# A two-group encoder step on one core: memory projections moved from the front into 64 steps that the recurrence and the latent attention are laid between, with half-size weight chunks

## The reference, cut to what matters

```python
p_mem_k = einsum('bmd,lde->lbme', mem_prompt, xa_wk)     # both layers, also outputs
p_mem_v = einsum('bmd,lde->lbme', mem_prompt, xa_wv)
z = x @ w_in                    # u, gate, c_q, c_kv, k_pe
u_c = causal_conv(u); h = rg_lru(u_c)                    # gates, decay, scan over time
rec_out = h * gelu(gate)
q = rms_norm(c_q) @ w_uq; ckv = rms_norm(c_kv)           # rope on q_pe and k_pe
attn_out = latent attention of q on ckv (w_uk, w_uv), chunk mask, softmax
x = layer_norm(alpha * x + concat(rec_out, attn_out) @ w_out)
x = layer_norm(alpha * x + cross_attention(x, p_mem_k[l], p_mem_v[l]))
x = layer_norm(alpha * x + squared_relu_mlp(x))
```

## Time and profile before

| what | value |
|---|---|
| timed runs | 3116.03, 3117.30, 3129.95 us, median 3117.3 |
| profiled execution, first to last instruction | 3119.3 us |
| TensorE busy | 3036.5 us (97%), 20530 matmuls |
| VectorE busy | 1907.7 us (61%) |
| ACT, POOL busy | 413.1 and 92.4 us (13% and 3%) |
| mean granted TensorE clock | 0.987 |

### The profile page before, as it was taken

One profiled execution on the slowest core, in us unless ns is written; L12 is line 12 of the kernel. 1 busy time (PEld: TensorE's weight loads), 2 busy tenths in 40 slices (PEclk: granted clock), 3 DMA queues, 4 the chain that ended last, 5 costly groups with the idle time before them and its releaser, 6 DMA issues.

```text
span 3119.3 us, 47921 instructions
## 1 busy us (share of the span) xinstructions
PE 3036.5 (97%) x20530; PEld 2862.2 (92%) x20530; DVE 1907.7 (61%) x1485; ACT 413.1 (13%) x763; POOL 92.4 (3%) x64
## 2 busy tenths in 40 slices
PE   8999999899999999999999998999999999999998
PEld 6888899689989899999999996898999999999997
DVE  5666667646635766555565668744676555566565
ACT  2000003310220211000110003311031100011001
POOL 0000000100000000000000001000000000000000
PEclk9999999889999999999999999999999999999999
DMA  6666654234344355555555552453445555555542
GB/s 240 223 218 212 225 179 109 99 111 158 126 144 135 120 163 161 164 168 166 162 161 162 161 166 78 152 162 122 148 135 161 163 167 167 161 163 162 163 160 71
DMA packets 432693, 489.03 MB, mean 157 GB/s; under 512 B 16802, under 2 KB 388280, under 8 KB 431224
## 3 DMA queue, kind: packets, MB, share of 16 engines
q1 hardware_dynamic: 421344, 453.01, 46.0%
q0 software_dynamic: 4432, 18.15, 1.7%
q10 hardware_dynamic: 6836, 16.73, 1.5%
HBM read 476.47 MB, written 11.40 MB: 156 GB/s over the span
## 4 chain that ended last, share of the span: by engine, by line
PE 90%; DVE 7%; ACT 1%; DMA 1%; issue 1%; DVEq 0%; ACTq 0%
PE ps L217 24%; PE ps L219 24%; PE ps L218 24%; PE ps L370 4%; PE ps L371 4%; PE ps L372 4%; DVE WL L1336 2%; DVE X L1575 1%; PE ps L433 1%; PE ps L713 1%; PE ps L689 1%; DVE XL L1570 1%; DVE WH L1334 1%; PE ps L585 1%; PE ps L680 0%
## 5 line engine op out<-in xcount | busy, mean ns | idle before, releaser
L217 PE MATMUL ps<-XH,WH 128*128 128x288 f32 x3760 | 1117.3, 297 | 27.6 <-DVE XL L1341 11.8
L219 PE MATMUL ps<-XH,WL 128*128 128x288 f32 x3760 | 1111.5, 296 | 0.0
L218 PE MATMUL ps<-XL,WH 128*128 128x288 f32 x3760 | 1111.0, 295 | 0.0
L1334 DVE CAST WH<-RAW 128x2048 fp32r<-128x2048 f32 x433 | 535.5, 1237 | 837.6 <-PE ps L219 718.3
L1336 DVE TENSOR_TENSOR WL<-RAW,WH 128x2048 fp32r<-128x2048 f32 x433 | 1020.8, 2358 | 14.9
L217 PEld LDWEIGHTS ps<-XH,WH 128*128 128x128 f32 x3760 | 708.1, 188 | 37.0 <-issue 16.7
L218 PEld LDWEIGHTS ps<-XL,WH 128*128 128x128 f32 x3760 | 708.3, 188 | 0.2
L219 PEld LDWEIGHTS ps<-XH,WL 128*128 128x128 f32 x3760 | 708.3, 188 | 0.0
L217 PE MATMUL ps<-HH,WH 128*128 128x288 f32 x2048 | 604.7, 295 | 1.7 <-DVE WL L1336 1.7
L219 PE MATMUL ps<-HH,WL 128*128 128x288 f32 x2048 | 604.3, 295 | 0.0
L218 PE MATMUL ps<-HL,WH 128*128 128x288 f32 x2048 | 603.9, 295 | 0.0
(11 more groups left out here) (252 smaller groups left out, 1514.1 us busy)
## 6 DMA issues: line engine op xcount, KB each, us to landing
RAW<-in_mlp_up SPq DMA_DIRECT2D x128, 1024.0 KB, 5.4
RAW<-in_mlp_down SPq DMA_DIRECT2D x128, 1024.0 KB, 5.3
RAW<-in_xa_wk SPq DMA_DIRECT2D x32, 1024.0 KB, 5.1
RAW<-in_xa_wv SPq DMA_DIRECT2D x32, 1024.0 KB, 5.1
RAW<-in_xa_wq SPq DMA_DIRECT2D x32, 1024.0 KB, 5.4
RAW<-in_xa_wo SPq DMA_DIRECT2D x32, 1024.0 KB, 5.3
RAW<-in_w_in SPq DMA_DIRECT2D x22, 1024.0 KB, 5.3
RAW<-in_w_out SPq DMA_DIRECT2D x16, 1024.0 KB, 5.3
```

Of the source, the lines that this page charges most:

```text
L217: nc.tensor.matmul(out, wh, xh, start=start, stop=False)
L218: nc.tensor.matmul(out, wh, xl, start=False, stop=False)
L219: return nc.tensor.matmul(out, wl, xh, start=False, stop=stop)
L1334: V.tensor_copy(WH[:, h, :], RAW[:, s, :]).then_inc(split_hi, 1)
```

## The change

- **Chunks of half the size.** A chunk is 512 KB (1024 numbers per partition). There are still four `RAW` slots, now half as large together; split slots go from two to four, and VectorE splits three chunks ahead (`AHEAD = 3`) where it split one ahead. Every `linear`, `down` and `pool` loop has twice as many loads, splits and waits for the same matmuls.
- **Input projection first.** x is loaded, transposed and split first, its transposes inside the first u block (`first_block`). Parameters are transposed after u. The memory rows are transposed after the input projection, alternating with the gate matmuls.
- **64 steps.** The memory projections (2 chunks to a step, 24 matmuls of 512 columns) are written out without a loop. Between them lie the pieces of the recurrence and of the latent attention, at step numbers written by hand: rms sums at 0, scans on VectorE at 7 to 14, `uq` in six chunks at 14 to 19, `uk` and `uv` in two halves at 23, 24 and 34, 35, attention units begun at 26 to 30 and 36 to 40 (scores at the unit's step, transposes two later, weighted sum three later). Steps 44 to 63 hold nothing but memory projections.
- **Work from POOL to VectorE.** The product with the input gate, the recurrent output and its low part.
- **Buffers.** The results of recurrence and attention have their own tiles (`RECH`, `RECL`, `ATTH`, `ATTL`), since `XH` and `XL` are taken by the split memory rows. `STG` has one buffer for both halves. The load of the sample's memory values `VS` is issued earlier. POOL starts loading keys only when the last memory projection is stored.

```diff
-CHUNK_ELEMS = 2048
-RAW_SLOTS, SPLIT_SLOTS = 4, 2
+CHUNK_ELEMS = 1024
+RAW_SLOTS, SPLIT_SLOTS = 4, 4
+AHEAD = 3
...
+    STEPS = 64
+    UQ_AT, UK_AT, UV_AT = 14, (23, 34), (24, 35)
+    UNITS_AT = (26, 36)
...
+        first_block()
+        linear_body("u", 0, blocks=(1,))
+        linear_body("u", 1)
...
+        for r in range(8):
+            mem_tile(r)
+            for n in (2 * r, 2 * r + 1):
+                if n >= 2:
+                    pe.wait_ge(sem("gates_sig"), n - 1)
+                nc.tensor.matmul(ps[:, 6 + n % 2, 0:CW], GW[:, n, :], UC[:, n % LT, 0:CW], start=True,
+                                 stop=True).then_inc(sem("gate_mm"), 1)
...
+        for s in range(STEPS):
+            mem_step(s)
+            if s == 0:
+                latent_sums()
...
+            if UQ_AT <= s < UQ_AT + 6:
+                queries(s - UQ_AT)
...
+            for n in range(NU):
+                if s == unit_at(n):
+                    mla_scores(n)
+            for n in range(NU):
+                if s == unit_at(n) + 2:
+                    mla_turn(n)
+                if s == unit_at(n) + 3:
+                    mla_sum(n)
...
         def ln(name, l, s, sums, following=None, high=True, pooled=False):
             if following:
-                split(PHASES[following], 1)
+                split(PHASES[following], AHEAD)
...
-            split(PHASES[f"wo{l}"], 1)
+            split(PHASES[f"wo{l}"], AHEAD)
             for n in (2, 3, 4):
                 low(n)
```

More of the change, by code:

```diff
@@ L123, in build @@
[L123 to L133, removed]
+    XIN = area("XIN", [P, 3, D], 37120)
@@ L296, in _ @@
                 for g in range(4):
-                    load(PHASES["pool"], g, 0, 0, kt_view(a["pool_w"][0][g]))
+                    for h in range(2):
+                        load(PHASES["pool"], 2 * g + h, 0, 0, kt_view(a["pool_w"][0][g])[:, :, 256 * h:256 * h + 256])
             linear(f"wq{l}", kt_view(a["xa_wq"][l]), 4)
@@ L458, in _ @@
+        linear_body("u", 1)
+        pe.wait_ge(sem("par_in"), 16 * 12)
         pe.wait_ge(sem("xT_low"), NK)
[L459 to L461 removed]
+        for t, rows in enumerate((96, 96, 118)):
+            last = nc.tensor.transpose(ps[:, 4, t * 128:t * 128 + rows], PN[0:rows, t, :], ID[0:rows, 0:rows])
+        last.then_inc(sem("parT"), 1)
+        for i in range(2):
             linear_body("gate", i, before=("u_out", 2))
[L463 removed]
+        linear_body("cq", 0, before=("gate_out", 2))
@@ new lines, in _ @@
+        c0 = PHASES["ckv"]
+        pe.wait_ge(sem("cq_out0"), 1)
+        for q in range(4):
+            pe.wait_ge(chunk_split, c0 + q + 1)
+            chunk_mms((c0 + q) % SPLIT_SLOTS, 0, lambda k: normed(4 * q + k), q == 0, q == 3).then_inc(chunk_used, 1)
+        c0 = PHASES["kpe"]
+        pe.wait_ge(sem("cq_out1"), 1)
+        for q in range(2):
+            pe.wait_ge(chunk_split, c0 + q + 1)
+            h = (c0 + q) % SPLIT_SLOTS
+            for k in range(8):
+                w = slice(k * P, (k + 1) * P)
+                last = product(ps[:, 2, 0:T], WH[:, h, w], WL[:, h, w], XH[:, 8 * q + k, :], XL[:, 8 * q + k, :],
+                               q == 0 and k == 0, q == 1 and k == 7)
+            last.then_inc(chunk_used, 1)
@@ new lines, in swap_halves, with keys_up @@
+        def swap_halves():
+            pe.wait_ge(sem("stateT_out"), 1)
+            for n in range(4):
+                last = nc.tensor.matmul(ps[:, 4 + n, 0:T], PERM, QP[:, n, :], start=True, stop=True)
+            last.then_inc(sem("swap"), 1)
+        def keys_up(g):
+            c = CHUNK["uk", g, 0]
+            h = c % SPLIT_SLOTS
+            pe.wait_ge(chunk_split, c + 1)
+            if g == 0:
+                pe.wait_ge(sem("ck_low"), 1)
+                pe.wait_ge(sem("roped"), 1)
+            else:
+                pe.wait_ge(sem("mla_ol"), 5)
+            for n in range(4):
+                for k in range(2):
+                    w = slice(k * 512 + n * P, k * 512 + n * P + P)
+                    last = product(ps[:, 4 + n, 0:KEYS], WH[:, h, w], WL[:, h, w], CKH[k][:, 0:KEYS],
+                                   CKL[k][:, 0:KEYS], k == 0, k == 1)
+            last.then_inc(chunk_used, 1)
@@ L1202, in _ @@
         act.wait_ge(sem("stored"), 16 * 13)
-        for half in range(2):
-            act.wait_ge(sem(f"mem_stored{half}"), 16 * 8)
+        act.wait_ge(sem("mem_stored"), 16 * 16)
     @block.gpsimd
@@ L1724, in _ @@
         pooled_x(0)
-        split(PHASES["pool"], 2)
+        for j in (4, 5):
+            split(PHASES["pool"], j)
         difference(2)
```

1144 lines of the change are left out of this document (607 added, 537 removed).

## The result

The change makes the kernel faster: 3069.77 us in the median of four runs (3067.59 to 3070.52) against 3119.23 us, a ratio of 0.9839, 95% interval 0.9821 to 0.9857. The forecast was 3072 us, with 3060 to 3098 as its range.

What follows compares the result with a forecast made beforehand. TensorE bounds the kernel (90% of the span), so time is won only where it idles or runs slowly. Gains less costs summed to 45 us off the 3119.3 us span, 3072 us against the median, range 3060 to 3098.

Steps and rivals of the forecast that it cites:

- The attention: Latent attention up to `wout`: full clock between memory steps instead of 0.70, gain 18 us, with 1.1 of waits 19.1.
- the start: Kernel start: 1.8 us gained from less idle time, 1.5 lost on memory transposes among the gates, 0.3 net.
- behind the front: Layers after the attention: earlier half splits remove waits behind LayerNorms and cross-attention and shorten `ln`'s split, gain 9 us.
- LayerNorm ends: Four LayerNorms that feed projections: the 0.96 us wait for the third chunk's split goes, gain 3.8 us.
- ends of the cross-attention: Two places where a whole-chunk split delays the low parts: a half split comes 1.7 us sooner, gain 3.4 us.
- The shorter split in `ln`: Split that `ln` does for the next phase: it gets shorter, partly on the path, gain 2 us.
- The backlog: Memory steps 3 to 13: VectorE falls 6.5 us behind and TensorE just begins to wait, cost 1 us.
- The seams: Some 40 pieces set between memory steps: cost taken as 0; a quarter microsecond at each would be 10.
- rival B: Memory steps 26 to 49: fp32 pieces pull the clock low, about 172 us lost, 3244 us; chance 0.03.
- the uq stretch: 540 to 574 us: split waits and half clock, put down to POOL's product, go; gain 14.2 us, 17.9 with nearby waits.
- Rival A: Seams 10 us, backlog 4, gates 5, only 5 behind the front: gain about 25 us, 3092; chance 0.15.
- Rivals C and D: C: late half-chunk loads bind, far above 3400 us, chance 0.02. D: errors cancel the gain, within 0.5%, chance 0.06.

Runs made afterwards that it cites:

- e1_packed: Changed kernel with all ten attention units and the second halves of uk and uv moved behind step 63, no memory steps between them: 3104.5 us.
- e3_lead2: Changed kernel with VectorE splitting two half chunks ahead instead of three: 3085.3 us.
- e8_start2: Changed kernel with one half chunk loaded beside x, tables and parameters issued from SP behind the fifth, 33 matmuls on constants while waiting: 3063.4 us.
- e12_before_dve2: Kernel before with recurrent output (behind the fourth uq split) and its low part on VectorE, ACT's high-part copy placed later: 3112.8 us against 3117.6.
- e4_pool: Changed kernel with the input product, the recurrent output and its low part given back to POOL: 3068.4 us.
- e7_raw2: Changed kernel with two load slots instead of four: 3112.6 us.
- e2_half: Changed kernel with a memory step at only every second of the 18 places from 26 to 43, the others later: 3083.2 us.

## Why the prediction was right, step by step

It came out near the middle, but with terms that were off in both directions: that the sum landed so near is in part luck.

**Right.** The attention: 19.2 us for 19.1, its clock 0.99, and bare again in e1_packed it cost 18.0 by slower matmuls. `uq` and the pieces around it: 17.7 for 17.9. The first `wout` matmul was forecast near 625 us and stands at 626.6. No wait for a split appeared; in the steps the smallest margin between a split and its use was 1.16 us at step 14, for a forecast of "just begins to wait near step 13", VectorE having fallen 4.8 us behind where I had 6.5. The half cast took 0.693 us for 0.70. x came at 12.90 us for 13. Of the earlier trace rows nothing is left: no such wait behind a LayerNorm, and 0.22 us at the end of the cross-attention. Behind the four LayerNorms the split is ready 0.68 us ahead of its use, the thinnest margin of the kernel.

**Mis-sized: the start, 2.7 for 0.3.** I had priced handing the memory transposes back and forth, but not their speed: among the gates they took 4.7 us, 1.1 of it a wait and 0.11 each, where at the start of before they had taken 8.3, 1.7 of it a wait and 0.21 each.

**Mis-sized: behind the front, 18.7 for 9.** Set side by side matmul for matmul, the LayerNorm ends gave 4.8 (forecast 3.8), as each wait of 0.96 cost 1.20 with the start of the next matmuls. The ends of the cross-attention gave 3.3 and 0.6 (3.4); 1.7 of the first is a clock that had gone low behind the wait. The shorter split in `ln` gave 0.9 (2), and the pool stage lost 0.5 (1). Two things were not in the sum at all. The first is 2.2 us of `wout`'s first matmuls, which still ran at 1.2 GHz behind the attention. The second is ten waits of some 0.43 us at the ends of blocks, 0.69 each with what follows, 6.9 us. They have the very cause that I had found at 549.7 us: POOL adds up residuals and, at all ten, the subtract beside it stretches to some 4.65 us. Before, and after, each around the first of the ten; in the fence of before the third row is the matmul that waits:

```profile
715.84 3.52 POOL L1254 TENSOR_TENSOR ACC<-X 128x1152 f32<-128x1152 f32 x1 [49.93 <-DVE X L1530]
716.85 4.66 DVE L1336 TENSOR_TENSOR WL<-RAW,WH 128x2048 fp32r<-128x2048 f32 x1
...
721.56 0.40 PE L217 MATMUL ps<-XH,WH 128*128 128x288 f32 x1 [0.44 <-DVE WL L1336]
```

```profile
678.58 2.99 POOL L1356 TENSOR_TENSOR ACC<-X 128x1152 f32<-128x1152 f32 x1 [39.94 <-DVE X L1699]
679.06 3.59 DVE L1439 TENSOR_TENSOR WL<-RAW,WH 128x1024 fp32r<-128x1024 f32 x1
```

The stretch is still there, ten times, 3.59 us instead of 1.23, but three halves of lead cover it. Two cover it as well: in e3_lead2 the ten subtracts are as long and nothing waits there. The view of waits had said so all along: 16 waits for `WL` with 16.4 us outside the memory projections, of which I priced two (8.4) and four (3.8) and left ten without asking.

**Mis-sized: the steps, 4.9 lost for 1.** The backlog cost nothing. The seams, which I had set at 0, cost 3.3: the first memory matmul behind a piece takes 0.31 to 0.46 us to the next instead of 0.227, some twenty times. And behind the first sample unit the clock fell, as in part of rival B, though for 3.3 us and not for 172:

```profile
429.44 0.40 PE L709 MATMUL ps<-PT,VV 32*128 32x32 f32 x2
429.77 0.50 PE L428 MATMUL ps<-WH,MTH 128*128 128x512 f32 x1
...
431.40 0.63 PE L428 MATMUL ps<-WH,MTH 128*128 128x512 f32 x1
```

Seven matmuls in a row stand 0.427 us apart, 1.6 us lost against e8_start2, where the clock stayed up. The same eight small matmuls behind step 43 did nothing; over the experiments it happened behind the one, the other, both or none.

**Right sum, part of the cause: the uq stretch.** I put its late splits down to POOL's product and counted the move to VectorE and the cover together. e12_before_dve2 makes the move alone and gains 4.4 us of this stretch; 6.4 of its 8.4 us of split waits stay. e4_pool undoes the move under cover and loses nothing. So the memory steps, with the longer lead, won the 17.7 us, and the move by itself would have won 4.4 of them.

**The baseline.** I took the span as 2.0 us above the median; the profiled execution was 3.9 above. With a sum 8.2 us too small against the profile, this brought the forecast to within 2.2 us of the median. Rival A is out with its price: the seams cost 3.3 of its 10 and there was no backlog. B is left with the short fall above. Rivals C and D are out: half a chunk landed in 3.4 to 4.4 us, and it took two slots (e7_raw2) to make loads bind, at +43 us.

## What to carry to other kernels

Small matmuls that depend on softmax and copies are best laid between long runs of independent ones: here the clock gave some 18 us and, beside the bare order of e1_packed, 16 us of waits were hidden, and the two need different amounts of cover, so try both separately and read clock and waits, not the time. When a view lists sixteen waits for one thing, price all sixteen. An edit that moves a transfer moves its issue too, onto a queue where something may stand behind it.

## What the runs showed of the hardware

- A VectorE operation with two SBUF operands, or a CAST from SBUF, that starts while a POOL operation on SBUF runs, ends about when POOL ends plus its own usual time: at 279.81 us in e4_pool POOL had 4.56 us to go, the CAST usually takes 0.69, and it took 5.10; at 716.85 before, 2.51 + 2.29 = 4.80 against 4.66. The Trainium skill (SBUF — State Buffer, "Who interferes with whom") says that the two share a pair of ports, that the second to issue is blocked fully rather than slowed, and names both kinds of operation; the trace agrees.
- TensorE's clock can fall while it never idles. Bare attention stood at 0.70 to 0.79, and in some executions, not in all, the dense matmuls behind 2.6 us of matmuls of 32 columns ran at 1.2 GHz. It can also stay up through waits: in e2_half it was 0.99 with waits of up to 2.3 us. The Trainium skill (TensorE: Matmul & The Clock Gate, "HAM oscillation — how this bites in real kernels") tells of a clock that falls because TensorE waits between bursts; here what filled the time between the waits mattered more.
- Matmuls on a tile of constants, run while the first load is under way, had the clock at full speed from the first product on (in e8_start2 products stand 0.13 us apart from 14.42 us on, clock 1.00 from 12 to 20 us). In the changed kernel the first products stood 0.24 us apart until 21.8 us, and 0.13 behind. The clock column shows 1.00 there too (12.9 to 21.8 us), so at the very start the step between matmuls tells the speed, not the column.
- A short wait on TensorE cost more than its length: with the matmuls right behind it, 0.43 us cost 0.69 (ten times) and 0.96 cost 1.20 (four times), against the same matmuls of after, which don't wait.
